# Input rows loaded and turned in three parts, one lower weight tile made ahead of a wait, and the gate/up product run over two weight units at a time

## The reference

```python
def even_layer(x, g_norm, w_in, b_f, w_out):
    z = rms_norm(x, g_norm) @ w_in
    ...
    log_f = jax.nn.log_sigmoid(fa.astype(f32) + b_f.astype(f32))
    ya = forgetting_attention(hA(qa), hA(ka), hA(va), log_f)
    ...
    return x + y @ w_out
...
        hn = rms_norm_2(h, g_pre_ffn[l])
        gu = hn @ w_gate_up[l]
        ff = (jax.nn.silu(gu[..., :D_FF]) * gu[..., D_FF:]) @ w_down[l]
        h = h + rms_norm_2(ff, g_post_ffn[l])
```

## Time and profile before

| what | us |
|---|---|
| median of 3 runs | 778.29 |
| lowest and highest run | 777.49, 779.05 |
| the profiled execution's own time | 776.32 |
| span of its trace | 774.5 |

### The profile page before, as it was taken

One profiled execution on the slowest core, in us unless ns is written; L12 is line 12 of the kernel. 1 busy time (PEld: TensorE's weight loads), 2 busy tenths in 40 slices (PEclk: granted clock), 3 DMA queues, 4 the chain that ended last, 5 costly groups with the idle time before them and its releaser, 6 DMA issues.

```text
span 774.5 us, 12608 instructions
## 1 busy us (share of the span) xinstructions
PE 763.5 (99%) x5057; PEld 660.1 (85%) x5057; DVE 519.8 (67%) x775; ACT 411.8 (53%) x663; POOL 231.9 (30%) x182
## 2 busy tenths in 40 slices
PE   8999999999999999999999999999999999999997
PEld 7889987899877889987778888998888888888885
DVE  5746794675566657866557965788778677777453
ACT  6644447634587445344335545736767555555351
POOL 3031797660752000046009910126002111011010
PEclk9999999999999999999999999999999999999999
DMA  9897996387721664555545556440464656654751
GB/s 234 202 246 188 253 204 189 84 195 176 172 85 44 230 186 131 199 191 140 160 136 158 180 200 195 137 139 29 137 217 135 206 176 191 204 187 155 231 174 54
DMA packets 78140, 130.70 MB, mean 169 GB/s; under 512 B 4478, under 2 KB 28274, under 8 KB 77954
## 3 DMA queue, kind: packets, MB, share of 16 engines
q1 hardware_dynamic: 76640, 124.96, 56.1%
q0 software_dynamic: 1200, 4.83, 1.9%
q10 hardware_dynamic: 242, 0.11, 0.0%
HBM read 128.82 MB, written 1.06 MB: 168 GB/s over the span
## 4 chain that ended last, share of the span: by engine, by line
PE 97%; DVE 1%; DMA 1%; ACT 1%; issue 0%; SPq 0%; DVEq 0%; ACTq 0%
PE ps L1654 15%; PE ps L1658 15%; PE ps L1662 15%; PE ps L1713 10%; PE ps L1699 6%; PE ps L1695 6%; PE ps L1691 6%; PE ps L1714 5%; PE ps L1784 2%; PE ps L1800 2%; PE ps L1815 2%; PE ps L2171 1%; PE ps L2046 1%; DMA stage<-in_even_w_in 1%; PE ps L1998 1%; PE ps L2054 1%
## 5 line engine op out<-in xcount | busy, mean ns | idle before, releaser
L1004 DVE TENSOR_TENSOR w_lo<-stage,w_hi 128x1024 fp32r<-128x1024 f32 x224 | 296.8, 1347 | 154.3 <-ACT w_hi L661 153.4
L661 ACT ACTIVATE w_hi<-stage 128x1024 fp32r<-128x1024 f32 x230 | 240.1, 1061 | 233.4 <-PE ps L1662 107.5
L1713 PE MATMUL ps<-act_t,w_hi 128*128 128x512 f32 x352 | 122.3, 392 | 0.4 <-DVE act_t L1041 0.4
L1654 PE MATMUL ps<-w_hi,act_t 128*128 128x512 f32 (+1 forms) x368 | 100.4, 395 | 0.2 <-ACT act_t L688 0.2
L1714 PE MATMUL ps<-act_t,w_lo 128*128 128x256 f32 x352 | 98.5, 280 | 0.0
L1662 PE MATMUL ps<-w_lo,act_t 128*128 128x512 f32 (+1 forms) x368 | 96.5, 385 | 0.0
L1662 PEld LDWEIGHTS ps<-w_lo,act_t 128*128 128x128 f32 x368 | 68.1, 188 | 14.0
L1654 PEld LDWEIGHTS ps<-w_hi,act_t 128*128 128x128 f32 x368 | 66.5, 188 | 15.3 <-issue 2.5
L1658 PE MATMUL ps<-w_hi,act_t 128*128 128x512 f32 (+1 forms) x304 | 79.4, 384 | 0.0
L1713 PEld LDWEIGHTS ps<-act_t,w_hi 128*128 128x128 f32 x352 | 65.8, 187 | 15.0 <-issue 0.6
L1714 PEld LDWEIGHTS ps<-act_t,w_lo 128*128 128x128 f32 x352 | 66.5, 189 | 0.0
(11 more groups left out here) (382 smaller groups left out, 1167.3 us busy)
## 6 DMA issues: line engine op xcount, KB each, us to landing
stage<-in_even_w_in SPq DMA_DIRECT2D x62, 512.0 KB, 5.6
stage<-in_odd_w_in SPq DMA_DIRECT2D x48, 512.0 KB, 4.1
stage<-in_w_gate_up SPq DMA_DIRECT2D x44, 512.0 KB, 4.5
stage<-in_w_down SPq DMA_DIRECT2D x22, 512.0 KB, 4.5
stage<-in_even_w_out SPq DMA_DIRECT2D x16, 512.0 KB, 4.0
stage<-in_odd_w_out SPq DMA_DIRECT2D x16, 512.0 KB, 3.7
stage<-in_w_in SPq DMA_DIRECT2D x10, 512.0 KB, 4.0
stage<-in_w_out SPq DMA_DIRECT2D x8, 512.0 KB, 5.1
```

Of the source, the lines that this page charges most:

```text
L661: nc.scalar.activation(w_hi[:, u % RING, :], stage[:, u % RING, :], ACT.Copy).then_inc(hi_ready, 1)
L1004: nc.vector.tensor_tensor(w_lo[:, u % RING, :], stage[:, u % RING, :], w_hi[:, u % RING, :].bitcast(F32), ALU.subtract).then_inc(lo_ready, 1)
L1654: mm(out[:, b, :], a_hi(k)[:, tok[b]], hi[:, i, :], start=(k == 0), stop=False)
L1713: mm(out[m], hi[:, i, w[m]], both[:, :, k, :], start=(k == 0), stop=(k == KD - 1), skip_group_check=True)
```

## The change

x is loaded in three parts (columns 0 to 255, 256 to 511, 512 to 1023). PE turns two tiles before unit 0, two behind unit 0 and four behind unit 1. ACT and DVE make both halves of unit 0 before tiles 2 and 3, and unit 2 (ACT) and the lower part of unit 2 (DVE) before tiles 4 to 7. DVE makes the lower part of the last unit of ("qa", 0) before it waits for `f_ln`. The gate/up product takes two units at a time: the 512-column products of both, then the 256-column products of both; the row of factors stands between these two passes of units 2 and 3.

```diff
-            def load_x(c, arrived):
+            def load_x(first, last, arrived):
...
-            load_x(0, x_in)
+            load_x(0, 2, x_in)
...
                     if u == 1:
-                        load_x(1, x_rest_in)
+                        load_x(2, 4, x_next_in)
+                    if u == 2:
+                        load_x(4, KD, x_rest_in)
...
             hi_of_turned(0, 2, 0, COL_EVEN)
             hi_of_half(0, 0)
+            hi_of_half(0, 1)
             hi_of_turned(2, 2, 2, COL_EVEN + 2)
-            hi_of_half(0, 1)
             hi_of_half(1, 0)
             hi_of_half(1, 1)
             next_unit[0] = HALVED
+            split_hi(3)
             hi_of_turned(4, 4, 4, COL_EVEN + 4)
-            split_hi(3)
             act.wait_ge(x_in, 16 * NB)
+            act.wait_ge(x_next_in, 16 * NB)
             act.wait_ge(x_rest_in, 16 * NB)
             squares(0, lambda b: x[:, b, :], lambda b: junk[:, b, :])
             split_hi(5)
...
             lo_of_half(0, 0)
+            lo_of_half(0, 1)
             lo_of_turned(2, 2, 2, COL_EVEN + 2, KD + 2)
-            lo_of_half(0, 1)
...
+            split_lo(3)
             lo_of_turned(4, 4, 4, COL_EVEN + 4, KD + 4)
...
             then(TS(f_in, f_in, 0.0, None, ALU.min))
+            split_lo(chunks[("qa", 1)][0])
             dve.wait_ge(f_ln, 1)
...
-            turn_x(0)
+            turn_rows(lambda b, k: x[:, b, k * P:(k + 1) * P], 2, 0)
...
                 if j == 0:
+                    pe.wait_ge(x_next_in, 16 * NB)
+                    turn_rows(lambda b, k: x[:, b, k * P:(k + 1) * P], 2, 2, 2)
+                if j == 1:
                     pe.wait_ge(x_rest_in, 16 * NB)
                     turn_x(4)
...
-            def ffn_unit(name, j, there=always):
+            def ffn_two_units(name, first, there=always, between=None):
...
+                ks = range(first * 2, first * 2 + 4)
+                for j in range(first, first + 2):
+                    hi, _ = unit_of(name, j)
+                    for i, k in enumerate(ks):
+                        there[1](k)
+                        for m in range(2):
+                            mm(ffn_result(name[1], j % 2)[:, m, :, :], hi[:, i, w[m]], both[:, :, k, :], start=(k == 0), stop=(k == KD - 1), skip_group_check=True)
+                if between:
+                    between()
+                for j in range(first, first + 2):
+                    _, lo = unit_of(name, j)
+                    lower_there(name, j)
+                    for i, k in enumerate(ks):
+                        for m in range(2):
+                            ins = mm(ffn_result(name[1], j % 2)[:, m, 0, :], lo[:, i, w[m]], act_t[:, k, :], start=False, stop=(k == KD - 1), skip_group_check=True)
+                    ins.then_inc(unit_used, 1)
...
-                for j in range(4):
-                    ffn_unit(("ffn", c), j, after_lo(3 * KD + 24) if c == 0 else always)
-                    if (c, j) == (0, 2):
-                        row_of_diag()
+                for j in (0, 2):
+                    ffn_two_units(("ffn", c), j, after_lo(3 * KD + 24) if c == 0 else always, row_of_diag if (c, j) == (0, 2) else None)
```

More of the change, by code:

```diff
@@ L260, in build @@
         drained = [sem("chunk_drained_even"), sem("chunk_drained_odd")]
+        x_next_in = sem("x_next_in")
         x_in, x_rest_in, ident_in, rows_in, late_in, masks_in, wf_in, b_in_landed, c_in_landed, tables_in, params_in = sem("x_in"), sem("x_rest_in"), sem("ident_in"), sem("rows_in"), sem("late_in"), sem("masks_in"), sem("wf_in"), sem("b_in_landed"), sem("c_in_landed"), sem("tables_in"), sem("params_in")
@@ L402, in _ @@
         def _(sp_eng):
-            def load_x(c, arrived):
-                half = slice(c * 512, (c + 1) * 512)
+            def load_x(first, last, arrived):
                 for b in range(NB):
-                    sp_eng.dma_start(x[:, b, half], t["x"][b * P:(b + 1) * P, half]).then_inc(arrived, 16)
-            load_x(0, x_in)
+                    sp_eng.dma_start(x[:, b, first * P:last * P], t["x"][b * P:(b + 1) * P, first * P:last * P]).then_inc(arrived, 16)
+            load_x(0, 2, x_in)
             for name, (first, units, per, _) in chunks.items():
@@ L1700, in channels_unit @@
                 ins.then_inc(unit_used, 1)
-            def ffn_unit(name, j, there=always):
-                hi, lo = unit_of(name, j)
+            def ffn_two_units(name, first, there=always, between=None):
                 both = act_t[:, :, :].rearrange("p (v k) n -> p v k n", v=2)
-                out = [ffn_result(name[1], j % 2)[:, m, :, :] for m in range(2)]
                 w = [slice(m * P, (m + 1) * P) for m in range(2)]
-                ks = range((j // 2) * 4, (j // 2) * 4 + 4)
-                lower_there(name, j)
-                for i, k in enumerate(ks):
-                    there[1](k)
-                    for m in range(2):
-                        mm(out[m], hi[:, i, w[m]], both[:, :, k, :], start=(k == 0), stop=(k == KD - 1), skip_group_check=True)
-                        ins = mm(out[m][:, 0, :], lo[:, i, w[m]], act_t[:, k, :], start=False, stop=(k == KD - 1), skip_group_check=True)
-                ins.then_inc(unit_used, 1)
+                ks = range(first * 2, first * 2 + 4)
[14 more added lines that the diff above has]
+                    ins.then_inc(unit_used, 1)
             x_hi = lambda k: act_t[:, k, :]
```

## The result

The changed kernel takes 780.94 us in the median of 7 executions (780.71 to 782.51), the kernel before, beside it, 778.29 in the median of 7 (776.33 to 779.54): ratio 1.0046, 95% interval 1.0026 to 1.0066, so slower, by 2.65 us. In four later jobs the kernel before took 776.2 to 776.8 in medians of 17 to 29 executions, so its seven here lie high, and 2.65 understates the loss. The profiled execution of the changed kernel is one of the longer ones: 782.46 us, span 780.7. The profiled one of before is the shortest of its seven, 776.3. Both facts matter further down.

A forecast was written before the change was run, and what follows sets the result against it. PE was taken as the bound, busy for 99% of the span and holding 97% of the chain. Start +2.7, forget gate -1.5 and row +2.0 gave +3.2 us, added to the median 778.3: 781.5, range 779.2 to 783.6.

The forecast's parts named there:

- First weight product at 7.1: Start: smaller x loads let unit 0's weights land sooner, so PE's first weight product begins at 7.1, not 7.74.
- the sum of 3.8: Total in us if 1 KB rows land no sooner and PE starts at 7.74; otherwise 3.2.
- What comes later, +2.7: Start: later turning delays ACT, so PE begins unit 3 at 20.0 instead of 17.26, +2.7 us.
- the claim that nothing adds up behind unit 3: Start: row of factors, its diag and the next units keep their order, so nothing is added to the +2.7.
- Forget gate, -1.5: Forget gate: lower part made in DVE's idle time, with 0.9 us cover, removes PE's wait, -1.5 us.
- Pace, 0: Gate/up product: grouping gains nothing at 0.347 us a pair; 0, within 0.3 over 352 pairs.
- The rival of a faster grouped product: Gate/up product, 352 pairs: grouped products run closer to the array's pace, at most 9.4 us saved, 772.1; chance 0.04.
- The row, +2.0: Ahead of chunk 1 of gate/up: later row and unit 2 release delay the copy to 599.77; PE waits, +2.0 us.
- The clock rival: Start: PE's clock falls in the new idle time, +1.8 us more, 783.3; chance 0.08.
- What the sum was added to: The +3.2 us was added to the 778.3 median of before, as the profiled 776.3 lay below all three timed runs.

The follow-up runs named there:

- part 1 alone: Kernel before with only the new start (x in three parts, tiles turned right before use): 778.65 us, ratio 1.0034.
- turning early: Changed kernel, row of factors copied before unit 6's lower part, tiles 2 and 3 turned before unit 0's product, 4 to 7 behind it: 775.97 us, ratio 0.9991.
- the two kernels with the row first: Changed kernel with DVE's copy of the row ahead of unit 6's lower part, 778.59 us; the same with the start of before, 775.39 us.
- the kernel with the filled wait: Changed kernel with ten 128-column products of ones ahead of PE's wait for the row of factors: 780.80 us, ratio 1.0050.
- the second run of part 2: Kernel before with only the forget gate's lower weight part made ahead of the wait for `f_ln`, run again: 775.05 us, ratio 0.9982.
- the last kernel: Kernel before with the early lower part at the forget gate and the row copied before unit 6's lower part, product still alternating: 774.93 us, ratio 0.9975.
- the changed kernel with the row first: Changed kernel with DVE's copy of the row of factors moved ahead of unit 6's lower part: 778.59 us, ratio 1.0024.

## Why the prediction was right, and where it was not

The forecast was 781.5 us with a range of 779.2 to 783.6 and slower as the likely case; measured 780.94. By its steps:

- **First weight product at 7.1:** began at 7.42. The weights were no longer what held ACT, as forecast: it takes both halves at 6.74 with no wait for a DMA. It was late because PE's transposes ended later, tiles 0 and 1 beginning at 6.01 where 5.68 was assumed; and by the spread of all profiles no gain of this kind is shown. The Trainium skill's page "Perfetto Trace Analysis", section "DMA Optimizations", warns of transfers under 2 KB. The first two loads of x, in before (rows of 2 KB) and in the changed kernel (rows of 1 KB), median us from issue to landing:

```profile
x<-in_x SPq DMA_DIRECT2D x2, 256.0 KB, 3.2
x<-in_x SPq DMA_DIRECT2D x2, 128.0 KB, 2.6
```

The quarter landed 0.6 us sooner, so the sum of 3.8 did not come about; for its bytes it took longer, so the page is not contradicted.

- **What comes later, +2.7:** each link held. Turning to ACT 0.63 (10.28 to 10.91), unit 1 at 12.32 (forecast 11.9), unit 2 at 16.43 (15.8), squares 2.08, unit 3 at 20.45 (20.0). Mis-sized by the 0.32 of the late beginning and by the claim that nothing adds up behind unit 3 (0.14 did): the row is +3.33. The start's loss is shown three times: in part 1 alone, by turning early, and by the 3.2 us between the two kernels with the row first.
- **Forget gate, -1.5:** the wait is gone, its cover is 0.75 us where 0.9 was forecast. From the first row to chunk 0 the changed kernel takes 1.32 less. That the wait itself is 0.5 to 1.3 us, by the execution, the forecast could not see in one trace.
- **Pace, 0:** off by a little: 0.348 a pair against 0.347, +0.4 to +0.5 us over 320 pairs. The lone paces of the earlier trace rows did not see it. The rival of a faster grouped product is out. The Trainium skill's page "TensorE: Matmul & The Clock Gate", section "Back-to-back issue gap", gives 0.216 us for 512 columns, as the gap of a lone product at the 2.4 GHz level; the traces have 0.229 in the grouped product. The forecast took that formula for a stream; it left it aside for the measured pace, rightly.
- **The row, +2.0:** +2.08 in the trace, 2.0 between the traces with and without it; the copy ended at 601.89, 2.1 behind the forecast 599.77, of which 2.0 is that chunk 0 began later.
- **The clock rival:** right that an idle stretch can lower the clock, right in size (1.8 forecast, 1.7 measured), wrong in place. At the start, with gaps of 1.45 and 1.02 us, nothing fell; behind chunk 0, after 1.90, it did in the profiled execution; by mean clock and time 3 of 7 are alike.
- **What the sum was added to:** the step that failed, though the number came out. Without the clock's fall the parts come to 3.33 - 1.32 + 2.08 + 0.4 = 4.5 us, not 3.2. The forecast added 3.2 to the median of before. But the profiled execution (776.3) has neither the slow pace nor a wait for the row, and others of the same kernel have both (779.33 in its second profile); that some of the seven behind the median do is inferred from their times, as they were not traced. 776.3 + 4.5 = 780.8 is what the changed kernel's shorter executions take. An underestimate of 1.3 us and a starting point 2.0 us above the execution that was read nearly cancelled, and that was luck. Against the 776.2 to 776.8 of the later jobs the change costs more than 4 us, not the 3.2 forecast; the kernel with the filled wait measured 4.4.

What stays open: what sets the pace of the alternating product (391 or 394 ns, or 399), and how much of the second group of times of the kernel before is this pace. The 24 pairs of chunk 0 ahead of the row take 8.40 us in before and 8.55 and 8.56 in the two executions with 399 ns, so the wait for the row does not cause the pace. But they take 8.54 in the second run of part 2 too, which then went on with 394 ns: the pace can change within an execution. That the twelve executions of the last kernel, the only alternating one with the old start and the row first, missed the slow pace by chance is possible and was not tested. Nor is every kernel with the row first so even: one execution of the changed kernel with the row first lies at 782.6, and those of the kernel that turns early are spread over 2.4 us. Nor was it traced why the clock falls behind the same wait in one execution and not in another.

## What to carry to other kernels

Deferring the preparation of an operand to right before its use costs nothing only if the engine that prepares it has slack behind that point. Here ACT idled 3 us and then was late for everything. When work is put between a product and the release of its buffer, follow the release through the in-order queues to what stands behind it: a copy of 0.42 us, put ahead of a weight part that nobody needed yet, was worth 2.0 us. And before a forecast is added to a median, look whether the profiled execution is a typical one, and how many executions the median stands on.

## What the hardware showed that I had not expected

- Two executions of one program, both at a granted clock of 1.00, run the same alternating 512- and 256-column products at 0.347 and at 0.353 us a pair: 2.2 us over 320 pairs.
- The granted clock halved for about 3.4 us behind an idle stretch of 1.90 us, in the middle of a kernel that had kept PE busy for 590 us, and not in every execution; with small products in the gap no mean clock was low in eight, and the one trace shows no fall.
- The waits of one kernel differ between its executions with the landing of its weights: ahead of chunk 1 none in one profile of the kernel before, 0.8 us in the other, where unit 6 landed late.
- A spread can hide two groups: of before's 25 executions in one job 17 lie within 2.6 us and the other 8 within 1.1 us, 1.6 us higher.
